# The widest level of the HGRN2 scores: eight products of 64 keys, or sixteen of 32

## The reference

```python
qe_rel = q * jnp.exp(b - b_ref)
ke_rel = k * jnp.exp(b_ref - b)
scores = jnp.einsum('bcthd,bcshd->bchts', qe_rel, ke_rel)
scores = jnp.where(mask, scores, 0.0)
o_intra = jnp.einsum('bchts,bcshv->bcthv', scores, v)
```

## Time and profile before

| | us |
|---|---|
| median of 3 runs | 1944.68 (1942.98 to 1945.22) |
| the profiled execution | 1943.6 |
| its span, first to last instruction | 1941.9 |
| TensorE busy, matmuls | 1932.7 |
| GpSimd busy | 905.8 |
| VectorE busy | 756.5 |
| ScalarE busy | 695.5 |

### The profile page before, as it was taken

The page is one execution under the profiler, slowest core; times in us unless marked ns, Lnnn a source line. Parts: engine busy times, 40 slices in busy tenths (PEclk is TensorE's granted clock), DMA queues, the critical chain, the costliest instruction groups (busy, mean ns, idle before and its releaser), DMA issues.

```text
span 1941.9 us, 28643 instructions
## 1 busy us (share of the span) xinstructions
PE 1932.7 (100%) x10408; PEld 1585.2 (82%) x10408; DVE 756.5 (39%) x1228; ACT 695.5 (36%) x965; POOL 905.8 (47%) x550
## 2 busy tenths in 40 slices
PE   9999999999999999999999999999999999999999
PEld 7888888888788888888888888888877888888887
DVE  6222221389875322231132222114888752222312
ACT  5222222364533322222332222224555433223223
POOL 3444444466335544444444444545653444444444
PEclk9999999999999999999999999999999999999999
DMA  5222333222113332333322233332221123222332
GB/s 187 98 98 97 93 99 97 90 77 80 64 55 98 108 97 97 96 90 99 107 88 98 97 97 92 91 102 88 73 89 56 65 89 117 97 97 89 95 99 97
DMA packets 53499, 181.75 MB, mean 94 GB/s; under 512 B 6816, under 2 KB 6816, under 8 KB 53408
## 3 DMA queue, kind: packets, MB, share of 16 engines
q1 hardware_dynamic: 53264, 180.56, 28.9%
q10 hardware_dynamic: 144, 0.00, 0.0%
HBM read 178.45 MB, written 2.10 MB: 93 GB/s over the span
## 4 chain that ended last, share of the span: by engine, by line
PE 92%; DVE 4%; issue 2%; ACT 1%; DMA 0%; DVEq 0%; SPq 0%; ACTq 0%
PE ps L1456 29%; PE ps L1458 29%; PE ps L1457 29%; PE ps L1578 1%; PE ps L1580 1%; PE ps L1579 1%; DVE w L1139 1%; PE ps L1773 0%; PE ps L1934 0%; DVE g L1002 0%; PE ps L1778 0%; PE ps L1757 0%; DVE e L1110 0%; DVE bf L1063 0%; DVE g L1008 0%
## 5 line engine op out<-in xcount | busy, mean ns | idle before, releaser
L481 POOL TENSOR_TENSOR wlo<-raw,whi 128x1024 fp32r<-128x1024 f32 (+1 forms) x536 | 903.5, 1702 | 1028.0 <-ACT whi L542 554.4
L1456 PE MATMUL ps<-hhi,whi 128*128 128x512 f32 x1760 | 692.0, 393 | 2.5 <-DVE wlo L877 1.6
L1458 PE MATMUL ps<-hhi,wlo 128*128 128x512 f32 x1760 | 685.4, 389 | 0.0
L1457 PE MATMUL ps<-hlo,whi 128*128 128x512 f32 x1760 | 685.1, 389 | 0.0
L1456 PEld LDWEIGHTS ps<-hhi,whi 128*128 128x128 f32 x1760 | 330.4, 188 | 80.8 <-issue 10.4
L1458 PEld LDWEIGHTS ps<-hhi,wlo 128*128 128x128 f32 x1760 | 330.4, 188 | 70.0
L1457 PEld LDWEIGHTS ps<-hlo,whi 128*128 128x128 f32 x1760 | 330.6, 188 | 66.5
L536 ACT ACTIVATE whi<-raw 128x1024 fp32r<-128x1024 f32 x168 | 177.2, 1055 | 280.2 <-PE ps L1458 258.2
L1456 PE MATMUL ps<-ahi,whi 128*128 128x512 f32 x704 | 273.9, 389 | 0.0
L1457 PE MATMUL ps<-alo,whi 128*128 128x512 f32 x704 | 273.9, 389 | 0.0
L1458 PE MATMUL ps<-ahi,wlo 128*128 128x512 f32 x704 | 273.9, 389 | 0.0
(11 more groups left out here) (264 smaller groups left out, 1365.1 us busy)
## 6 DMA issues: line engine op xcount, KB each, us to landing
raw<-in_up SPq DMA_DIRECT2D x168, 512.0 KB, 3.2
raw<-in_mix SPq DMA_DIRECT2D x64, 512.0 KB, 3.3
raw<-in_dn SPq DMA_DIRECT2D x64, 448.0 KB, 3.3
raw<-in_dn SPq DMA_DIRECT2D x32, 512.0 KB, 3.5
raw<-in_lead SPq DMA_DIRECT2D x8, 512.0 KB, 3.2
x<-in_x SPq DMA_DIRECT2D x8, 256.0 KB, 5.9
raw<-in_lead SPq DMA_DIRECT2D x8, 256.0 KB, 6.0
raw<-in_mix SPq DMA_DIRECT2D x8, 256.0 KB, 2.5
```

The lines of the kernel that those rows point to most:

```text
L481: low = pool.tensor_tensor(wlo[:, q, part], raw[:, q, part], whi[:, q, part].bitcast(F32), ALU.subtract)
L1456: mm(dst, whi[:, q, s], mh, start=start, stop=False)
L1457: mm(dst, whi[:, q, s], ml, start=False, stop=False)
L1458: return mm(dst, wlo[:, q, s], mh, start=False, stop=stop)
```

## The change

In the widest level each product of 64 keys by 64 queries becomes two products of 32 keys by 64 queries. The helper gets the number of keys, `m`, apart from the number of queries, `n`. The results land at the same places of PSUM. The semaphore is raised by the last product of each head as before.

```diff
--- before.py
+++ after.py
@@ -1654,32 +1654,33 @@
 
                 def hg_scores(p):
 
-                    def scores(c, h, s0, t0, n, keys, queries):
+                    def scores(c, h, s0, m, t0, n, keys, queries):
 
                         c0 = c * P
                         hh = slice(HALF * h, HALF * h + HALF)
-                        return mm(bank(5 + h)[s0:s0 + n, c0 + t0:c0 + t0 + n],
-                                  keys[p % 2][hh, c0 + s0:c0 + s0 + n], queries[p % 2][hh, c0 + t0:c0 + t0 + n],
+                        return mm(bank(5 + h)[s0:s0 + m, c0 + t0:c0 + t0 + n],
+                                  keys[p % 2][hh, c0 + s0:c0 + s0 + m], queries[p % 2][hh, c0 + t0:c0 + t0 + n],
                                   start=True, stop=True)
 
 
                     for c in range(TC):
                         for s0 in range(0, P, 2 * CH):
                             for h in range(2):
-                                scores(c, h, s0, s0, 2 * CH, e2, e1)
+                                scores(c, h, s0, 2 * CH, s0, 2 * CH, e2, e1)
                     for c in range(TC):
                         for s0 in range(0, P, 2 * CH):
                             for h in range(2):
-                                scores(c, h, s0, s0 + CH, CH, e4, e3)
+                                scores(c, h, s0, CH, s0 + CH, CH, e4, e3)
                     for c in range(TC):
                         for s0 in range(0, P, 4 * CH):
                             for h in range(2):
-                                scores(c, h, s0, s0 + 2 * CH, 2 * CH, w2, w2)
+                                scores(c, h, s0, 2 * CH, s0 + 2 * CH, 2 * CH, w2, w2)
                     for c in range(TC):
-                        for h in range(2):
-                            last = scores(c, h, 0, 4 * CH, 4 * CH, w1, w1)
-                            if c == TC - 1:
-                                last.then_inc(score.sem, 1)
+                        for s0 in range(0, 4 * CH, 2 * CH):
+                            for h in range(2):
+                                last = scores(c, h, s0, 2 * CH, 4 * CH, 4 * CH, w1, w1)
+                                if c == TC - 1 and s0:
+                                    last.then_inc(score.sem, 1)
 
                 def value(p, c, h):
                     return vt[:, c, P * p + HALF * h:P * p + HALF * h + HALF]
```

## The result

The changed kernel took 1955.17 us (median of 6 runs, 1953.36 to 1955.79) against 1944.95 us for the kernel before (6 runs): a ratio of 1.0052 [1.0041, 1.0063]. It is slower, as forecast, but by 10.2 us where 6.7 were forecast, and outside the range. Its profiled execution took 1953.73 us, 1.4 us less than the median, with a span of 1952.0 us at a mean granted clock of 0.997; the span of before was 1941.9 us at 1.00. One of the 18 executions of the kernel before that stand beside the first experiments took 3249.84 us at a mean granted clock of 0.555; it is left out of the ratios, which compare with the other 17.

A forecast was written before the change was run, and what follows sets the result against it. TensorE was taken to bound the kernel. From the profiled 1943.6 us, -1.1 direct and +7.8 for code stalls gave 1950.3 us; the runs' median being 1.1 us higher, the forecast was 1951.4 us, range 1943.4 to 1953.4 us.

The forecast's parts named there:

- the indirect cost: Shifted code position: TensorE stalls on late code blocks in each layer's third and fourth score-product groups, 7.8 us in all.
- the holes: TensorE stalls awaiting code: 1.8 us in each layer's third dense score-product group, 2.1 us in its fourth.
- the direct part: Widest level of the score products: no tile-shape change before it, four tiles side by side; 0.14 us gained a group, 1.1 in all.
- Rival 1: Code blocks are fetched further ahead, so no new stalls in the score-product groups: 1943.6 us, not slower; chance 0.14.
- Rival 2: One of the two new stalls a layer in the score-product groups stays out or is short: 1947.8 us; chance 0.15.
- rival 3: Column tiles take turns in the widest level, 0.93 us a level, on top of the stalls: 1955.4 us; chance 0.05.
- The wait at line 1786: TensorE's wait for ScalarE, 0.3 us a layer, keeps its size, as TensorE itself releases both its ends.
- Nothing absorbs it: The new stalls, 7.8 us over both layers, show fully in the time, since TensorE waits for nobody.
- Group 1 keeps its hole: Each layer's first dense score-product group keeps its stall (0.36 and 0.26 us idle): its code-block boundary precedes the changed level.

The follow-up runs named there:

- second try: The changed kernel plus 134 already-met waits, 28, 22 and 84 ahead of each layer's first, second and third dense score-product groups: 1946.72 us, ratio 1.0011.

## Why the prediction was right, and where it was wrong

**The failed step: the indirect cost, "1.8 + 2.1 = 3.9 us a layer, 7.8 us in both", priced a hole at its length alone.** The clock behind a hole was put at nothing, without a reason and without a bound. The runs showed a second price: the clock is granted at 0.50 for 3.41 us behind three of the four new holes, in each of the two profiled executions of the changed kernel, at 1.6 us each. That is 4.8 us of the 10.1, and more than the whole miss of 3.8 us (1955.2 against 1951.4). No row of before showed the low level behind a hole; but its holes, of 0.36 and 0.26 us idle, say nothing of holes of 2 us. With 3 x 1.6 us the sum would have been 1956.2 us.

The miss is smaller than the missing term because small terms went the other way. Of the 3.4 us between the forecast's 1950.3 and the profiled 1953.7, the low clock is +4.8, the holes +0.25, the direct part -0.2, line 1786 -0.7, the start of the program and the return of the loop -0.75. The last three were put at nothing.

**The holes: right.** They came in group 3 at 407 instructions (after matmul 203) and group 4 at 306 (after matmul 153), in both layers, with 1.93 / 1.86 us for the 1.8 forecast and 2.07 / 2.19 us for the 2.1. The fetches started 1.74 and 1.80 us after group 3's start (forecast 1.6) and 0.99 and 1.14 after group 4's (0.7 to 1.2; by the prediction's own numbers, 1.5 less 96 x 0.0042, the upper end is 1.1). The code came 2.3 to 2.4 us after its fetch's start, where 2.6 less some 0.1 was taken, so two small errors offset each other in group 3. Rival 1 (no new hole) fell with the first profile, and the 96 instructions of filling showed the cause: holes at the same places with the old products. Rival 2 (one hole out) fell too. The 22 instructions ahead of group 4 made nearly that case, and its profiled execution, with the clock at 1.00 throughout, took 1947.2 us for the forecast's 1947.8; that is in part luck, as the median of the ten runs is 1949.0.

The Trainium skill (Runtime: NRT & Kernel Launch, Instruction fetch mechanics) has the cost of crossing a block of code "mostly hidden". By that rule there would be no new holes. The trace agrees where the code runs slowly, where a group has one boundary, and where the first of two stands at 3, 8 or 17. Six holes of 0.5 to 2.2 us in one execution speak against it for a dense run of small products.

**The direct part: right, slightly small.** It is 0.16 us a group instead of 0.14. In the groups without a hole, from the last matmul of the level below to the first of the widest it was 122 ns and is 15; from the widest level's first to last start 463 ns and is 431 (forecast 430), and the contributions follow after 145 to 149 ns in both. These steps make the 0.14 us; the rest lies ahead of them, where the last matmul of the level below starts 17 ns sooner. So the four tiles of 64 rows by 32 columns run side by side, and rival 3 (they take turns, 0.93 us a level) is out. Its 1955.4 us is the time that was measured, and that is a coincidence. The table by shape after (busy us, mean ns | idle before), against the earlier trace rows:

```profile
L1661 PE MATMUL ps<-w 64*32 64x32 f32 x256 | 4.7, 197 | 4.6 <-issue 4.6
...
L1661 PE MATMUL ps<-w 64*32 64x64 f32 x256 | 5.3, 218 | 0.0
```

256 records take 5.3 us of busy time where 128 took 5.5.

**The wait at line 1786 "keeps its size": wrong, harmless.** The wait (line 1787 after) is gone in the first profile of the changed kernel and is 0.3 us once in the second. TensorE comes later by the holes, ScalarE does not; -0.7 us. That is a small absorption, and the prediction had said "Nothing absorbs it".

**Group 1 keeps its hole: right** (0.53 and 0.53 us from start to start for 0.55 and 0.45).

**Open.** What decides which hole of about 2 us lets the clock fall; what sets the start of a fetch to better than some 2 us (a boundary at 3 has it later than one at 8; eight instructions did not move it in group 1, seven moved it by 1.4 us in group 4, where the fillers' places changed a little too). And no version of the change beats the kernel before: the direct 1.3 us is in every group of the traces and was never seen in the time, since every shift of the code that freed a group brought idle time elsewhere.

## What to carry to other kernels

Every instruction added to TensorE is also code, and moves all code behind it. Before adding some to a kernel that TensorE bounds, count the instructions from one dense group to the next, lay the blocks of 256 over them, and look for two boundaries in one dense group, the first of them 16 or more instructions in. A group of 350 to 400 instructions at 4.2 ns each runs through a block in 1.1 us, while the code of a block came 2.2 to 2.7 us after its fetch's start. And price such a hole of 1.5 us or more at its length plus, in some three cases of five here, another 1.6 us of low clock.

## What was not expected of the hardware

- The granted clock fell to 0.50 behind idle places of 1.5 to 2.7 us, in the midst of a kernel in which TensorE was busy before and after: 12 of 20 in the groups, and none of the two of 1.51 us in the second try's projections. The stretches are 3.41 us long, twice 6.83.
- Which of the holes it follows changes from one execution to the next of the same kernel, with the time the same within 0.1% (1955.17 and 1955.14 us).
- Waits that are met already are not free on TensorE: 84 instructions of them in two projection blocks made steps of up to 0.47 us between products that usually follow each other after 0.23.
- The start of a fetch can jump: moving a boundary by 7 instructions, 0.03 us of code in the group or 0.8 us in the projections, changed it by 1.4 us (the seven fillers themselves are the other thing that differs).
